# Two transformer blocks on one Trainium2 core: squares of the norms added over feature tiles on VectorE before TensorE sums them

## What is computed

```python
def _rms_f32(xf, g):
    return xf * lax.rsqrt(jnp.mean(xf * xf, axis=-1, keepdims=True) + EPS) * g.astype(jnp.float32)

h = h + mix.astype(h.dtype)
h = h + swiglu(rms_norm(h, ffn_norm[layer]), ffn_w_gate[layer], ffn_w_up[layer], ffn_w_down[layer])
```

## Time and profile before

| | |
|---|---|
| median of three runs | 1113.61 us (1112.51 to 1115.98) |
| the profiled execution | 1115.49 us, of which its span is 1113.7 us |
| PE busy | 1051.3 us, 94% of the span |
| DVE busy | 644.4 us, 58% |
| ACT busy | 506.8 us, 46% |
| mean granted clock of PE | 0.974 |
| read and written in device memory | 164 GB/s over the span |

### The profile page before, as it was taken

The page is one execution under the profiler, slowest core; times in us unless marked ns, Lnnn a source line. Parts: engine busy times, 40 slices in busy tenths (PEclk is TensorE's granted clock), DMA queues, the critical chain, the costliest instruction groups (busy, mean ns, idle before and its releaser), DMA issues.

```text
span 1113.7 us, 16603 instructions
## 1 busy us (share of the span) xinstructions
PE 1051.3 (94%) x7158; PEld 909.9 (82%) x7158; DVE 644.4 (58%) x709; ACT 506.8 (46%) x575; POOL 68.5 (6%) x84
## 2 busy tenths in 40 slices
PE   7998999999999997999999998999898879999997
PEld 6996888888888784988888887898557768888886
DVE  5656548666676552657776554353558654444544
ACT  6467454444445233644444443454456444444332
POOL 0001200000000000000010000000226000000000
PEclk9999999999999998899999999999989889999999
DMA  6541447666762774347788554222000335555451
GB/s 259 194 172 51 179 159 251 230 239 226 245 213 84 238 230 142 121 181 269 265 298 288 182 180 179 109 93 97 1 1 2 115 116 187 189 188 176 170 183 39
DMA packets 34046, 187.69 MB, mean 169 GB/s; under 512 B 3776, under 2 KB 8128, under 8 KB 15296
## 3 DMA queue, kind: packets, MB, share of 16 engines
q1 hardware_dynamic: 25920, 155.66, 39.5%
q0 software_dynamic: 7200, 27.27, 7.2%
q10 hardware_dynamic: 864, 3.88, 0.9%
HBM read 181.09 MB, written 1.05 MB: 164 GB/s over the span
## 4 chain that ended last, share of the span: by engine, by line
PE 86%; DVE 5%; ACT 4%; DMA 2%; issue 1%; SPq 1%; POOL 0%; DVEq 0%; ACTq 0%
PE PS L269 12%; PE PS L271 12%; PE PS L270 12%; PE PS L534 11%; PE PS L535 11%; PE PS L536 11%; PE PS L997 2%; DMA raw<-wstream 1%; PE PS L434 1%; PE PS L547 1%; PE PS L298 1%; PE PS L299 1%; PE PS L300 1%; DMA U<-CU 1%; ACT w_hi L252 1%
## 5 line engine op out<-in xcount | busy, mean ns | idle before, releaser
L256 DVE TENSOR_TENSOR w_lo<-raw,w_hi 128x2048 fp32r<-128x2048 f32 x140 | 320.6, 2292 | 223.3 <-ACT w_hi L252 223.3
L252 ACT ACTIVATE w_hi<-raw 128x2048 fp32r<-128x2048 f32 x141 | 269.1, 1911 | 209.4 <-PE PS L271 103.2
L534 PE MATMUL PS<-w_hi,a_hi 128*128 128x512 f32 x528 | 211.7, 401 | 4.4 <-DVE a_lo L460 4.2
L535 PE MATMUL PS<-w_lo,a_hi 128*128 128x512 f32 x528 | 208.2, 394 | 0.0
L536 PE MATMUL PS<-w_hi,a_lo 128*128 128x512 f32 x528 | 208.2, 394 | 0.0
L269 PE MATMUL PS<-a_hi,w_hi 128*128 128x256 f32 (+1 forms) x608 | 187.5, 308 | 15.5 <-DVE a_lo L1897 5.0
L271 PE MATMUL PS<-a_hi,w_lo 128*128 128x256 f32 (+1 forms) x608 | 182.9, 301 | 0.0
L270 PE MATMUL PS<-a_lo,w_hi 128*128 128x256 f32 (+1 forms) x608 | 182.8, 301 | 0.0
L269 PE MATMUL PS<-h_hi,w_hi 128*128 128x256 f32 x528 | 149.9, 284 | 0.4 <-DVE h_lo L699 0.4
L271 PE MATMUL PS<-h_hi,w_lo 128*128 128x256 f32 x528 | 149.4, 283 | 0.0
L270 PE MATMUL PS<-h_lo,w_hi 128*128 128x256 f32 x528 | 149.4, 283 | 0.0
(11 more groups left out here) (304 smaller groups left out, 1085.9 us busy)
## 6 DMA issues: line engine op xcount, KB each, us to landing
raw<-wstream SPq DMA_DIRECT2D x142, 1024.0 KB, 4.9
modraw<-wmod POOLq DMA_DIRECT2D x48, 512.0 KB, 5.0
U<-CU SPq DMA_DIRECT2D x32, 142.0 KB, 4.5
cst<-cst ACTq DMA_DIRECT2D x1, 1632.0 KB, 9.9
mlw<-mlw ACTq DMA_DIRECT2D x1, 1280.0 KB, 5.8
X<-xT SPq DMA_DIRECT2D x2, 512.0 KB, 5.3
CROW<-crow POOLq DMA_DIRECT2D x1, 1024.0 KB, 5.2
CTX<-ctxT POOLq DMA_DIRECT2D x1, 1024.0 KB, 8.5
```

The source lines that it names most:

```text
L252: nc.scalar.activation(w_hi[:, slot, :], raw[:, rslot, :], ACT.Copy).then_inc(S("hi_done"), 1)
L256: dve.tensor_tensor(w_lo[:, slot, :], raw[:, rslot, :], w_hi[:, slot, :].bitcast(F32), ALU.subtract).then_inc(S("lo_done"), 1)
L534: nc.tensor.matmul(out, a_hi[:, k, src, ts], wh, start=k == 0, stop=False, skip_group_check=True)
L535: nc.tensor.matmul(out, a_hi[:, k, src, ts], wl, start=False, stop=False, skip_group_check=True)
```

## The change

DVE adds tiles of squares in place before PE sums them.

- `fold_squares`: for n = 0 two adds (4 + 4 tiles, then 2 + 2), PE sums two tiles instead of four. For n = 1, 2, 3 three adds (4 + 4, 2 + 2, 1 + 1), behind the last `folded_lo`; PE sums one tile. For n = 1 and 3 that is 2 matmuls of one column instead of 16.
- `fold_pair`, for n = 4, 5, 6: an add of two tiles behind the third residual add and another behind the fourth. PE sums tiles 0, 1, 6 and 7, all behind the last unit, tiles 6 and 7 waiting for the fourth square.
- A new counter `sq_folded` orders the adds and releases PE.

```diff
-        def norm_pe(pe, n, quarters=range(4)):
-            for j in quarters:
-                pe.wait_ge(S("norm_sq"), 4 * n + j + 1)
-                if j == 0 and n > 0:
-                    pe.wait_ge(S("norm_rs"), n)
-                for k in (2 * j, 2 * j + 1):
-                    i = nc.tensor.matmul(PS[:, 6, 0:T], ones, SQ[:, k, :], start=k == 0, stop=k == KT - 1,
-                                         skip_group_check=True)
-                if j == 3:
-                    i.then_inc(S("norm_ss"), 1)
+        SQ_FOLDS = {0: 2, 1: 5, 2: 8, 3: 11, 4: 13, 5: 15, 6: 17}
+
+        def fold_squares(dve, n):
+
+            for i, w in enumerate((4, 2, 1) if n else (4, 2)):
+                first = i == 0
+                dve.wait_ge(*((S("norm_sq"), 4 * n + 4) if first else (S("sq_folded"), SQ_FOLDS.get(n - 1, 0) + i)))
+                dve.tensor_tensor(SQ[:, 0:w, :], SQ[:, 0:w, :], SQ[:, w:2 * w, :], ALU.add).then_inc(S("sq_folded"), 1)
+
+        def fold_pair(dve, n, j):
+
+            dve.wait_ge(S("norm_sq"), 4 * n + j + 1)
+            if j == 2:
+                dve.wait_ge(S("sq_folded"), SQ_FOLDS[n - 1] + 1)
+            dve.tensor_tensor(SQ[:, 0:2, :], SQ[:, 0:2, :], SQ[:, 2 * j:2 * j + 2, :], ALU.add).then_inc(S("sq_folded"), 1)
+
+        def norm_pe(pe, n):
+            if n:
+                pe.wait_ge(S("norm_rs"), n)
+            pe.wait_ge(S("sq_folded"), SQ_FOLDS[n])
+            tiles = {0: (0, 1), 2: (0,)}.get(n, (0, 1, 6, 7))
+            for k in tiles:
+                if k == 6:
+                    pe.wait_ge(S("norm_sq"), 4 * n + 4)
+                i = nc.tensor.matmul(PS[:, 6, 0:T], ones, SQ[:, k, :], start=k == 0, stop=k == tiles[-1],
+                                     skip_group_check=True)
+            i.then_inc(S("norm_ss"), 1)
 
         def norm_tokens_pe(pe, n):
 
             pe.wait_ge(S("norm_rs"), n)
+            pe.wait_ge(S("sq_folded"), SQ_FOLDS[n])
             for t in range(2):
-                for k in range(KT):
-                    pe.wait_ge(S("norm_sq"), 4 * n + k // 2 + 1)
-                    i = nc.tensor.matmul(PS[:, 6, t:t + 1], SQ[:, k, t * P:(t + 1) * P], ones[:, 0:1], start=k == 0,
-                                         stop=k == KT - 1)
+                i = nc.tensor.matmul(PS[:, 6, t:t + 1], SQ[:, 0, t * P:(t + 1) * P], ones[:, 0:1], start=True, stop=True)
             i.then_inc(S("norm_ss"), 1)
...
                     i.then_inc(S("x_updated"), 1)
+                if sums and j > 1:
+                    fold_pair(dve, sums, j - 1)
             if behind is not None:
                 folded_lo(dve, behind, 3)
+                fold_squares(dve, behind)
...
-            dve.wait_ge(S("norm_sq"), 4)
-            dve.tensor_tensor(SQ[:, 0:4, :], SQ[:, 0:4, :], SQ[:, 4:8, :], ALU.add).then_inc(S("sq_halved"), 1)
+            fold_squares(dve, 0)
             lo(dve, 1)
```

More of the change, by code:

```diff
@@ L501, in out_units_pe @@
                     pe.wait_ge(S("x_updated"), 4 * update + j - 1)
-                if sums and j == 3:
-                    norm_pe(pe, sums, (0, 1))
                 outs = [PS[:, 4 + j % 2, nb * T:(nb + 1) * T] for nb in range(2)]
-                feature_unit(u % SLOTS, outs, src, (lambda k: wait_act(pe, event, k)) if j == 0 else None,
-                             (lambda: norm_pe(pe, sums, (2,))) if sums and j == 3 else None)\
+                feature_unit(u % SLOTS, outs, src, (lambda k: wait_act(pe, event, k)) if j == 0 else None)\
                     .then_inc(S("unit_done"), 1)
             if sums:
-                norm_pe(pe, sums, (3,))
+                norm_pe(pe, sums)
         PAIRS = FT // 2
@@ L572, in down_last @@
                         i.then_inc(S("down_done" if nb < 7 else "unit_done"), 1)
-                    if sums and nb == 5:
-                        norm_pe(pe, sums, (0,))
                 if sums:
-                    norm_pe(pe, sums, (1, 2, 3))
+                    norm_pe(pe, sums)
             def turn(i, o, last=False, first=False):
@@ L680, in mod_rows, with ffn_dve @@
                                      op0=ALU.mult, op1=ALU.add, accum_out=MOD[:, n, c:c + 1]).then_inc(S("mod_done"), 1)
-        def ffn_dve(dve, f, gate=None, folded=False, behind=None, between=None, mods=None):
+        def ffn_dve(dve, f, gate=None, folded=False, behind=None, between=None, mods=None, sums=None):
             u0 = U_FFN[f]
@@ L811, in first_sums @@
                 pe.wait_ge(S("cst_loaded"), 16)
[L812 to L815, removed]
+                norm_pe(pe, 0)
             def factor_columns():
@@ L1818, in _, with residual_units @@
             dve.wait_ge(S("lo_done"), U_OUT1 + 3)
-            def residual_units(u0, add, norm=None):
+            def residual_units(u0, add, norm=None, sums=None):
                 if u0 != U_OUT1:
@@ L1831, in residual_units @@
                     folded_lo(dve, norm, 3)
+                    fold_squares(dve, norm)
             def plain(j):
@@ L1923, in _ @@
             ffn_dve(dve, 1, folded=True, mods=40,
-                    between=context)
+                    between=context, sums=4)
             norm_dve(dve, 4, lambda k: GSC[:, 0, k:k + 1], lambda k: MOD[:, k, 0:1])
@@ L2146, in gated @@
                 i.then_inc(S("x_updated"), 1)
-            residual_units(U_OUT2, gated)
+            residual_units(U_OUT2, gated, sums=5)
             norm_dve(dve, 5, lambda k: GSC[:, 2, k:k + 1], lambda k: MOD[:, 24 + k, 0:1])
-            ffn_dve(dve, 2, lambda k: MOD[:, 40 + k, 0:1])
+            ffn_dve(dve, 2, lambda k: MOD[:, 40 + k, 0:1], sums=6)
             norm_dve(dve, 6, lambda k: prm("fing", k), split=False)
```

## The result

The changed kernel took 1098.54 us in the median of six executions (1097.48 to 1100.6). The kernel before, executed beside it, had a median of 1113.06 us (six executions), 14.5 us more; the recorded ratio of the two is 0.9855, 95% interval 0.9833 to 0.9877, which is 16 us (14 to 19). I had forecast 12.7 us and a range of 1097.5 to 1106. The direction was right and the gain was forecast too small. Over four sets of executions on four chips the kernel before has a mean of 1114.81 us (78 executions, +-0.37) and the changed one, over its own four sets, 1099.94 us (24, +-0.48): 14.9 +-0.6 us. With the 12 executions of before_again the first mean is 1114.93.

What follows compares the result with a forecast made beforehand. PE bounds the kernel (94% busy, 86% of the chain). Gains of 0.87 + 1.84 + 3.04 + 4.72 + 0.5 + 1.75 + 0.0 = 12.7 us from 1113.61 give 1100.9, say 1101 us; range 1097.5 to 1106.

Steps and rivals of the forecast that it cites:

- the price of the records: PE's sums: each removed record of 256 columns gives 0.217 us, each of one column 0.108 us.
- DVE's adds: Three dependent in-place adds at n = 1 to 3 cost DVE 1.25 + 0.71 + 0.43 = 2.4 us.
- the rival of slow adds: In-place adds each 0.5 us slower, losing time at n = 1 and 3 to 6: 1106 us; chance 0.05.
- The wait at n = 1: PE reaches the sums of n = 1 early and waits 1.3 us for DVE's adds; gain there 1.8 us.
- The pauses of 2.5, 1.7 and 1.7 us: At n = 4 to 6, PE pauses 1.8 to 2.4 us after the last unit, then does 8 records.
- The order at n = 4: DVE's fourth residual add queues behind a new add and ends late; gain 0.5 of PE's 2.2 us.
- the clock behind n = 3: Unit after n = 3 no longer falls to low clock once one-column matmuls go: 1.69 us, making n = 3 4.7.
- my two sums: Whole gain 12.7 us if one-column work causes the clock fall behind n = 3, 11.0 if the fall comes back.
- The clock falls elsewhere: New PE pauses ahead of the sums at n = 1, 4 and 6 lower the clock: +2 to +6 us, 1103 to 1107; chance 0.16.
- late behind n = 3: Weights for a unit after n = 3 land 1 to 2 us later, eating 1.7 us: 1102.6; chance 0.10.
- Gains were given back: Gains of n = 0 and n = 2 lost in waits at attention and convolution: 3.9 us, 1105; chance 0.08.
- How the numbers follow: Step setting chances (forecast 0.58, faster 0.92) and the range 1097.5 to 1106 from clock rival and runs' spread.

Runs made afterwards that it cites:

- before_again: The kernel before, unchanged, executed and profiled a second time; ratio 1.0007 (0.9983 to 1.0031).
- cols14: Changed kernel with 14 more one-column matmuls at n = 3, results unused; 1107.06 +-0.69 us, ratio 0.9934.
- wide7: Changed kernel with 7 more 256-column matmuls at n = 3, results unused; 1104.83 +-1.10 us, ratio 0.9913.
- first_four: Changed kernel with n = 4, 5 and 6 as before, only n = 0 to 3 folded; the first four gave 9.9 +-1.0 us.
- first_four_again: Second set of the kernel with n = 0 to 3 folded and n = 4 to 6 as before; its profile took 1096.38 us at clock 0.988.
- best: Changed kernel with pairs folded early at n = 1, nothing folded at n = 4, only the first pair at n = 5 and 6; ratio 0.9866.
- best2: As the other version without the waits for DVE, but at n = 1 one fold stands ahead of the weight split; 1099.35 +-0.79 us, ratios 0.9841 and 0.9880.

## Why the prediction was right and wrong

**Right: the price of the records, and what stays late behind each.** 0.217 us for a record of 256 columns and 0.108 for one of one column gave n = 0, 2 and n = 3's records to within 0.03 us. DVE's adds were taken at 2.4 us for three and took 2.40; no add was slow, and the rival of slow adds falls. The wait at n = 1 (1.40 us) and none at n = 2 and 3 are those of the text. The pauses of 2.5, 1.7 and 1.7 us ahead of 8 records at n = 4, 5 and 6 lie just outside its 1.8 to 2.4. The order at n = 4 is as forecast: DVE's fourth residual add between two adds of squares sets the end, 2.5 us earlier on PE and 0.62 in the factor, where the clock holds.

**Right: the clock behind n = 3.** It was argued from one row; cols14 against wide7 shows it. By the Trainium skill (TensorE: Matmul & The Clock Gate, Part 1) the clock follows how busy the array has lately been. The profile calls PE equally busy in both kinds of records, and the clock fell behind one of them alone. Of my two sums, 12.7 and 11.0, the row's stood at this place.

**The rivals.** *The clock falls elsewhere* came in part. In the pair profiled for the result nothing of it is seen: the low stretch behind n = 4 is 663 to 667 us, as at 677 to 681 before. But over all profiles the clock fell at the 8 records behind the 2.51 us pause in seven of nine, and "against" it I had only one row with a shorter pause, 1.33 us. The price was 0.4 to 1.5 us in the records (forecast 1.7) and 1.4 us in all on average, at n = 4 alone; the pauses of 1.66 us at n = 5 and 6 show none. The same page of the Trainium skill (Why this matters for your kernels) warns of idle gaps between bursts: behind the gap of 2.51 us the traces agree in seven of nine executions, behind those of 1.66 us the fall it warns of did not come. This loss makes the gain smaller, so it is not why the gain was forecast too small. The weights were not late behind n = 3: PE went through the units after it without a wait. Gains were given back only in part: at the transfers of the convolution PE waits longer. All of this line in before and in after:

```profile
PE PS L997 <- DMA U<-CU: 3.6, 3, 1.9
```

```profile
PE PS L1007 <- DMA U<-CU: 4.3, 3, 2.5
```

It is 3.6 to 5.1 us in the three profiles with n = 1 and 2 as before (mean 4.2), 4.3 to 6.7 in the four of the changed kernel (mean 5.1): some 0.9 us seems to go back there, with single executions up to 2.4 us apart. I had set this rival at 3.9 or nothing.

**Wrong: the step "How the numbers follow".** Two things failed in it. First, the term for the clock away from the norms: the sum counts the clock only where I had seen a cause, n = 3, and takes every other place at 1.2 GHz of the one profiled execution for fixed, a term of nothing for which no reason was given. They were 20.4 us of "lost" time, more than the whole gain, and they wander: elsewhere than at n = 1 and 3 between 8.7 and 23.6 us in 17 profiled executions. The forecast had them as a danger on one side (new pauses, +2 to +6 us) and allowed one low stretch fewer on the other, though places that come and go can go by several. In the pair profiled for the result the two attentions gave 6.1 us, and all that lies outside the norms 5.2. Second, the range below the forecast was "the runs' own spread of 1.1 to 2.4 us", from three executions, "with a low stretch fewer" (1.7). Taken in full these give 1096.8, not 1097.5. Executions of the kernel before lie 6 us below and above their mean, and the lower bound of 1097.5 lies 1.5 us above the best execution of the changed kernel (1096.0). With those 6 us below it the range would have begun at 1095.

**How much of the 14.9 us is explained.** 12.8 at the norms of the pair, -0.9 at the convolution's transfers, and -0.8 for the low clock at n = 4 that the pair did not have (2.3 us lost on average in the changed kernel, 1.5 in that profile): 11.1. The other 3.8 us come for the most part with a mean clock that is higher than n = 3 and n = 4 would make it. Span less "lost" bears this out: 1089.9 and 1092.2 us in the two profiles of before, 1080.9 to 1082.7 in the four of the changed kernel, 9.4 us between the means where ledger and transfers, without the clock at n = 3, have 10.4. So nothing is missing outside the clock. Within it, n = 1 adds a little to the mean but brings no time, since it is waited away in w_lo. Why the rest of the clock is higher stays open. It hangs on no norm that was tried alone, the parts add up to 9.6 +-1.4 or 12.3 +-1.7, and the low places elsewhere took 13 to 18 us in the four profiles of the changed kernel and 17 to 24 in the four of kernels with n = 3 as before: a difference that the chance seen in first_four and first_four_again (17.9 and 8.7 in the same kernel) is large enough to make.

## What to carry to other kernels

- Price a removal from the distance of its records in the stream and then ask who is late next; where both were read from rows, each norm of the profiled pair came out within 0.25 us, also where an add on another engine took the place of the wait.
- Before an outcome is put at a few microseconds, add up what the execution loses to a low clock outside the change. If it is more than the forecast, it belongs into the range on both sides, and a profiled pair can't be differenced without taking it out.
- Look at a new pause of TensorE in more than one execution. The pair profiled for the result shows no fall of the clock behind the 2.51 us at n = 4, and seven of nine executions do.
- When work is moved to the idle time of an in-order engine, put it ahead of the instruction that waits and not behind: what is queued after it pays otherwise (best against best2).

## What the runs showed of the hardware

- TensorE's granted clock falls to its lower level behind 3.0 to 3.5 us of one-column matmuls, for about 3.5 us, in five profiled executions of five; behind as long a stretch of 256-column matmuls it stays at 1.00 (one execution). The four records of one column that are left cost nothing of it at n = 3 (twelve of twelve).
- Behind a pause of 2.51 us between two stretches of matmuls the clock fell at the next 8 records in seven executions of nine (2.40 to 3.44 us instead of 1.97); behind the pauses of 1.66 us at n = 5 and 6 it did not in nine of nine; with no pause, in the same place, it did not in three of three (best, best2).
- Places at 1.2 GHz in the short-matmul stretches (attention, convolution) come and go from execution to execution of the same program on the same chip. With them the time moves by about 0.8 to 1.0 us per 0.001 of mean granted clock, over 12 us in all in 78 executions of the kernel before.
- Three dependent in-place adds on DVE (1024, 512, 256 columns) take 2.40 us; their own medians are 1.23, 0.69 and 0.42, 2.34 in sum, so they follow one another with some 0.03 us between. Adds of 512 columns that don't depend on one another start 0.60 us apart on the same engine, though each takes 0.69 (656.20, 656.81 and 657.41 us at n = 4). So a dependent add comes some 0.1 us later than an independent one would.
